# A mixed projection's seven products kept in one slot, instead of two of them being issued in the next slot

## The reference

```
n = rms_norm_2(h, mix_norm_g[l])
q, k, v, qi, ki, wi, xr, yg, cv, gt = split(n @ w_in[l])
attn = dsa_attention(...)             # index scores, top-k, softmax attention
rnn  = rg_lru_branch(xr, yg, ...)     # short conv, gates, scan
cnv  = conformer_conv_branch(cv, ...) # 31 taps, layer norm, silu
g_attn, g_rnn, g_conv = split(sigmoid(gt))
merged = g_attn * (attn @ w_o_attn) + g_rnn * (rnn @ w_o_rnn) + g_conv * (cnv @ w_o_conv)
h = h + merged @ w_out
h = h + (silu(f @ w_gate) * (f @ w_up)) @ w_down      # f = rms_norm_2(h, ffn_norm_g[l])
```

## Time and profile before

| | |
|---|---|
| time, median of 3 runs | 1772.97 us (1772.41 to 1773.33) |
| the profiled execution: its own time | 1771.53 us |
| its span, first to last instruction | 1769.7 us |
| TensorE busy | 1710.7 us, 97% of the span |
| VectorE busy | 1123.0 us, 63% |
| GpSimd busy | 620.6 us, 35% |
| ScalarE busy | 544.5 us, 31% |
| mean granted clock of TensorE | 0.987 |

### The profile page before, as it was taken

One profiled execution on the slowest core, in us unless ns is written; L12 is line 12 of the kernel. 1 busy time (PEld: TensorE's weight loads), 2 busy tenths in 40 slices (PEclk: granted clock), 3 DMA queues, 4 the chain that ended last, 5 costly groups with the idle time before them and its releaser, 6 DMA issues.

```text
span 1769.7 us, 35538 instructions
## 1 busy us (share of the span) xinstructions
PE 1710.7 (97%) x14578; PEld 1457.2 (82%) x14578; DVE 1123.0 (63%) x2020; ACT 544.5 (31%) x1218; POOL 620.6 (35%) x553
## 2 busy tenths in 40 slices
PE   6999998899999999999999999999999997999999
PEld 3344654898888988877899999989888887999999
DVE  2225435566457878979657664368888887667643
ACT  2122236344343355432422010143454304130100
POOL 0002300564106313204644555245123036545652
PEclk9999999899999999999999999999999999999999
DMA  8322300000144434433344444444343343445543
GB/s 323 128 95 95 119 24 1 3 4 4 67 176 143 146 129 156 142 115 125 120 147 164 167 161 158 162 147 161 119 146 121 139 147 116 151 165 172 172 164 108
DMA packets 53377, 225.68 MB, mean 128 GB/s; under 512 B 5088, under 2 KB 29024, under 8 KB 29280
## 3 DMA queue, kind: packets, MB, share of 16 engines
q1 hardware_dynamic: 53216, 223.40, 36.5%
HBM read 222.34 MB, written 1.05 MB: 126 GB/s over the span
## 4 chain that ended last, share of the span: by engine, by line
PE 88%; DVE 6%; ACT 2%; DVEq 1%; issue 1%; DMA 1%; SPq 0%; ACTq 0%
PE PS L748 18%; PE PS L705 15%; PE PS L1013 14%; PE PS L2528 9%; PE PS L1037 8%; PE PS L2025 2%; DVE arena L1420 2%; PE PS L2038 2%; PE PS L687 1%; PE PS L2621 1%; PE PS L865 1%; DMA ring<-stream_dram 1%; PE PS L828 1%; PE PS L977 1%; PE PS L843 1%
## 5 line engine op out<-in xcount | busy, mean ns | idle before, releaser
L748 PE MATMUL PS<-arena,ring 128*128 128x272 f32 (+1 forms) x1664 | 390.0, 389 | 0.4 <-DVE arena L1648 0.4
L748 PEld LDWEIGHTS PS<-arena,ring 128*128 128x128 f32 x1664 | 311.6, 190 | 59.8 <-issue 6.1
L1420 DVE SCALAR_TENSOR_TENSOR arena<-arena,par 128x272 f32<-128x272 f32 (+1 forms) x480 | 258.7, 597 | 6.7
L1860 POOL TENSOR_TENSOR arena<-ring 128x512 f32<-128x512 f32 x48 | 68.8, 1433 | 444.5 <-DMA ring<-stream_dram 355.6
L705 PE MATMUL PS<-arena,ring 128*128 128x136 f32 (+1 forms) x1536 | 202.2, 280 | 1.3 <-ACT arena L1123 1.3
L705 PEld LDWEIGHTS PS<-arena,ring 128*128 128x128 f32 x1536 | 192.9, 191 | 8.0 <-ACT arena L1123 1.7
L2528 PE MATMUL PS<-arena,ring 128*128 128x512 f32 (+2 forms) x448 | 158.2, 514 | 1.7 <-DVEq L2851 1.7
L1013 PE MATMUL PS<-arena 128*128 128x136 f32 (+1 forms) x1280 | 152.1, 277 | 0.0
L705 PE MATMUL PS<-arena 128*128 128x136 f32 (+1 forms) x1152 | 147.8, 280 | 4.3 <-ACT arena L1103 3.0
L1013 PEld LDWEIGHTS PS<-arena 128*128 128x128 f32 x1280 | 148.7, 191 | 0.0
L2528 PEld LDWEIGHTS PS<-arena,ring 128*128 128x128 f32 (+1 forms) x448 | 84.0, 189 | 75.0 <-issue 69.5
(11 more groups left out here) (394 smaller groups left out, 2759.7 us busy)
## 6 DMA issues: line engine op xcount, KB each, us to landing
ring<-stream_dram SPq DMA_DIRECT2D x185, 1024.0 KB, 4.9
ring<-stream_dram SPq DMA_DIRECT2D x32, 512.0 KB, 4.0
ring<-stream_dram SPq DMA_DIRECT2D x16, 384.0 KB, 3.9
arena<-x_dram SPq DMA_DIRECT2D x1, 2048.0 KB, 11.7
cst<-const_dram SPq DMA_DIRECT2D x1, 1080.0 KB, 7.7
out_dram<-H SPq DMA_DIRECT2D x4, 256.0 KB, 3.4
cst<-const_dram SPq DMA_DIRECT2D x1, 912.0 KB, 10.1
arena<-stream_dram SPq DMA_DIRECT2D x1, 512.0 KB, 8.0
```

The costliest lines, as they stand in the source:

```text
L748: last = mm(PS[:, 2 * (j % 2) + f, nw], w[:, k, P * f:P * f + P], src[:, k, nw], start=k == 0, stop=k == KD - 1)
L1420: stt(CVG[:, c, NQ], CVA[:, c, j + Q0:j + T2], dw_w[l][:, c, j:j + 1], CVG[:, c, NQ], ALU.mult, ALU.add)
L1860: g.tensor_tensor(to[:, 0], w21, w22, ALU.add).then_inc(L["summed"], 1)
```

## The change

All seven products of a mixed slot are issued in that slot. TensorE's list in it is now a, g, c, h, then what `within(j)` holds, then e, b, d, in both layers. Exactly one other product stands between a copy and the product that reads on: `g` between `a` and `c`, `c` between `g` and `h`, `h` between `c` and `e`, `b` between `e` and `d`. On ScalarE the copies of `e` and `d` go to the end of the slot, behind all of its other work. VectorE's and GpSimd's lists are as before. The wait for the fourth conv half moves with `e` from slot 43 to slot 42.

```
-        PRODUCTS = counted([[("a", j), *last_parts(j - 1, "e"), ("g", j), ("c", j), *last_parts(j - 1, "d"), ("b", j)]
...
+        PRODUCTS = counted([[(name, j) for name in (("a", "g", "c", "e", "b", "d") if j in MIXED else ("f0", "f1"))]
+                            for j in range(MIXES)])
...
                 if j in MIXED:
                     product_a(j)
-                    if j == OC_J + 1:
-                        pe.wait_ge(L["conv_halves"], B["conv_halves"] + 4)
-                    if j - 1 in MIXED:
-                        product_e(j - 1)
...
                     product_c(j)
-                    if j - 1 in MIXED:
-                        product_d(j - 1)
+                    product_h(j)
                     within(j)
-                    product_h(j)
+                    if j == OC_J:
+                        pe.wait_ge(L["conv_halves"], B["conv_halves"] + 4)
+                    product_e(j)
                     product_b(j)
+                    product_d(j)
...
                 else:
-                    plain(j, 0, range(4))
-                    if j - 1 in MIXED:
-                        product_e(j - 1)
-                    plain(j, 0, range(4, 8))
-                    if j - 1 in MIXED:
-                        product_d(j - 1)
+                    plain(j, 0, range(8))
                     within(j)
                     plain(j, 1, range(8))
-            product_e(MIXES - 1)
-            product_d(MIXES - 1)
...
                 if j in MIXED:
                     copy_a(j)
-                    if j - 1 in MIXED:
-                        copy_e(j - 1)
                     copy_g(j)
                     copy_c(j)
-                    if j - 1 in MIXED:
-                        keep_d(j - 1)
...
                 if j >= WO_J + 2:
                     gain(j - 2)
+                if j in MIXED:
+                    copy_e(j)
+                    keep_d(j)
             gain(MIXES - 2)
-            copy_e(MIXES - 1)
-            keep_d(MIXES - 1)
             gain(MIXES - 1)
```

More of the change, by code:

```diff
@@ L417, in counted @@
             return {key: i + 1 for i, key in enumerate(key for row in rows for key in row)}
-        def last_parts(j, *names):
-            return [(name, j) for name in names if j in MIXED]
         def f0_at(j):
@@ L429, in f1_at @@
             return 2 * MIXED.index(j) + 2
-        PRODUCTS = counted([[("a", j), *last_parts(j - 1, "e"), ("g", j), ("c", j), *last_parts(j - 1, "d"), ("b", j)]
[L433 to L439, removed]
+        PRODUCTS = counted([[(name, j) for name in (("a", "g", "c", "e", "b", "d") if j in MIXED else ("f0", "f1"))]
+                            for j in range(MIXES)])
+        COPIES = counted([[(name, j) for name in (("a", "g", "c", "e", "d") if j in MIXED else
+                                                  () if j in BRANCH or j >= WO_J else ("f0", "f1"))]
+                          for j in range(MIXES)])
         LAYER_COUNTS = dict(
@@ L1239, in scalar_layers @@
                     copy_a(j)
-                    if j - 1 in MIXED:
-                        copy_e(j - 1)
                     copy_g(j)
                     copy_c(j)
-                    if j - 1 in MIXED:
-                        keep_d(j - 1)
[L1246 to L1252, removed]
+                elif j not in BRANCH and j < WO_J:
+                    keep_plain(j, 0)
                 if j in (GA_J, GA_J + 1):
```

## The result

The changed kernel takes 1801.78 us (median of 4 runs, 1801.19 to 1803.0) against 1772.89 us before, a ratio of 1.016 with a 95% interval of 1.0146 to 1.0174: 28.9 us slower. The profiled execution has a span of 1801.1 us, 31.4 us more than before; the difference of the medians is smaller, since the profiled execution of before lies 1.4 us under its median and that of after (1803.0 us) 1.2 over.

The account below looks back on a forecast made before the run. TensorE, busy 97% of the span, was taken as the bound. Terms 8.3 + 10.5 + 0.9 + 3.4 - 1.1 = 22.0 us, plus 2.4 for the clock, on 1771.53 gave 1796; with 1.44 for the median, 1797.5 us; range 1786 to 1804.

Parts of the forecast that it names:

- The formula from rows of before: Wait of d for ScalarE's work beyond the free cover, slots 5 to 24: 8.3 us layer 0, 10.5 layer 1.
- One product between a copy and its reader: All mixed slots: costs nothing where ScalarE is free, with 0.40 of 0.93 us to spare.
- Waits added ahead are not paid back: Against the rival that waits in slots 39 and 37 shrink by all they have: -8.7 us, 1789, chance 0.13.
- The entry of the list: TensorE's total wait behind the copy of e: from 1.3 to about 20 us, longest 3 to 4 us.
- The step on slots 5 and 7: d waits for the rectifier and squares in slot 5, 1.3 us, and the sigmoid in slot 7, 0.65; both layers.
- that rival: ScalarE is held longer at a table load than its row says, with a copy queued behind: 1811, chance 0.01.
- I expect the clock to stay up: -1.6: Slots 38 to 42, layer 0: d cuts the 2.57 us pause in pieces, so 1.6 us of lost clock is saved.
- I take two falls at 1.2: +2.4: Clock falls after new waits in slots 24, 40 and 42: 2.4 us in all, bounds 0 and 8.
- My rival of the clock: Clock falls at each wait of 2 us and more (slots 11, 24, 40, 42): 8.0 us, 1803, chance 0.13.
- 1.1 us for b as a cover: End of both layers, slot 49: b covers d's wait for e's copy, -1.3 us, less 0.2 for the gains.
- My bound for the gains: Gains of slot 48 coming behind d's copy, end of a layer: bounded at 0 to 1.3 us, taken at 0.2.
- c of slot 42 was to wait for the copy of a: Slot 42's copies queue behind d's copy of 41, held until slot 40 is gated: +0.9 us layer 0, +3.4 layer 1.

Follow-up runs that it names:

- experiment 1: Changed kernel with the copy of e moved ahead of or into ScalarE's other work in the nine slots where d waited: 1783.86 us, ratio 1.0058.
- experiment 2: Changed kernel with e and d of those nine slots issued in the next slot, as before the change: 1783.3 us, ratio 1.0047.
- experiment 4: Changed kernel with the buffer of a mixed slot's weights given back as late as before the change: 1800.17 us, ratio 1.0145.
- experiment 3: Kernel before with slot 24 alone changed: 1781.24 us, ratio 1.0045.
- experiment 9: Changed kernel, e's copies earlier, buffers held, slots 41 to 44 in old order, slot 48's gain earlier, GpSimd waiting for VectorE's squares: 1770.47 us, ratio 0.9985.
- experiment 6: Kernel before with slot 49 alone changed, and the gain of slot 48 between the copies of e and d there: 1773.82 us.
- experiment 5: Kernel before with slot 49 alone changed: 1774.76 us.
- experiment 8: Kernel of experiment 6 with slot 41's copy of a and slot 40's copy of e taken after the fourth of eight silu: 1775.36 us, ratio 1.0013.

## Why the prediction was right, and where it was not

The forecast was 24.5 us slower, the result is 28.9. Its mechanism is the one that acts, and its size is off by terms that partly cancel: 9.2 us that I had too low against 2.4 that I had too high. Without the 2.4 the time would have come out at 1804, the edge of my range, so that it lies 2 us inside it is in part luck.

**Right as it stood.** ScalarE's other work ahead of the copy of e makes d wait, in the nine slots named and in no other (experiments 1 and 2). The formula from rows of before gave 3.15 and 3.65 us for slot 24, and the listed waits with 0.27 added are 3.16 and 3.64; 1.75 and 1.75 for slots 18 and 21 of layer 1, measured 1.75 and 1.73; 0.9 for slots 18 and 21 of layer 0, measured 0.71 and 0.69; 2.05 for slot 11 of layer 0, of which 0.65 is paid back in slot 13, measured 1.78 + 0.27 = 2.05 and a step of 1.21. One product between a copy and its reader costs nothing where ScalarE is free. Waits added ahead are not paid back in slot 37 of layer 1 (5.97 us against 6.14). The entry of the list was to grow to about 20 us and grew to 29.0, 9.6 of it in slots 38 to 40.

**The step on slots 5 and 7.** I wrote of slot 5 that c's copy "stays there (as many products lie ahead of it as before)". That was wrong: d of the slot before now lies ahead of it too, and the copy came at 576.09, not 574.92 (0.24 of these 1.17 us came from ahead of slot 2, the other 0.93 is that product). In slot 5 of layer 0 this cancelled, since the rectifier moved with it (1.26 us against 1.3). But VectorE's scores hang on the rectifier, and the sigmoid of slot 7 on VectorE: it was not fixed in time, as I took it. In layer 1 the rectifier waits 0.80 us for VectorE, so that slot 5 lost 2.00 us and not layer 0's 1.3. Slot 7 lost 1.90 and 1.75 us where I had 0.65. Part of that is a second thing, in the timeline of the changed kernel:

```profile
591.02 1.27 POOL L1840 TENSOR_TENSOR ring<-ring 128x512 f32<-128x512 f32 x1
591.07 1.37 DVE L1508 TENSOR_TENSOR arena<-arena 128x136 f32<-128x136 f32 x1
...
592.52 1.28 ACT L1159 ACT_TABLE_LOAD   x1 [1.92 <-DVE arena L1508]
...
593.81 0.66 ACT L1159 ACTIVATE arena<-arena 128x544 f32<-128x544 f32 x1
```

VectorE's addition, on which the sigmoid waits, took 1.37 us beside GpSimd; with the buffers held (experiment 4) it took 0.29, and the wait was 0.37 us shorter. Together the two slots account for 3.0 us of what was missed. The sigmoid again starts 0.01 us after its table load, so that rival stays out.

**The clock.** "I expect the clock to stay up: -1.6" came true, the fall behind slot 39 went. "I take two falls at 1.2: +2.4" was mis-sized: four new ones came, in slots 24 and 40 of both layers, and lost 8 us together. In slot 24 they cost 4.84 - 3.16 = 1.7 and 6.46 - 3.64 = 2.8 us; experiment 3 shows them with slot 24 changed alone (4.74 - 3.16 = 1.6 and 5.32 - 3.64 = 1.7). In slot 40 they lost 1.7 us each; the wait in slot 42 that was to hide them isn't there, and they are part of the step from 38 to 47. Slot 24 alone is 2.1 us over the whole term. My rival of the clock, with 8.0 us and 1803, was nearer in size than the forecast: four of its five falls came and cost as much. Its rule doesn't hold, though: the wait of 2.31 us in slot 37 of layer 0 left the clock at 1.00.

**What I left out.** I followed the copies and not the ring. d in its own slot frees the weights' buffer earlier, the transfer and GpSimd's sums of weights come earlier, and before slot 37 of layer 0 they fall on VectorE's taps: 2.6 us (experiment 4). At the end of a layer I credited 1.1 us for b as a cover; it came out at a loss of 0.4, because TensorE, 0.95 us earlier there (the old wait of 0.68 at d, and 0.27), releases GpSimd into VectorE's additions (experiment 9). My bound for the gains was beside the point (experiment 6).

**Too high.** c of slot 42 was to wait for the copy of a, 2 to 3 us in layer 1. In the changed kernel it doesn't wait at all; in experiments 1 and 2, with the waits at d gone, it waits 3.2 to 3.7 us. The queue behind the copy of d of 41 is real, but VectorE gated slot 40 early enough in the changed kernel. Its last addition there in layer 1, first before, then after:

```profile
1506.19 1.60 DVE L1648 TENSOR_TENSOR arena<-arena 128x512 f32<-128x512 f32 x1
```

```profile
1533.30 0.69 DVE L1623 TENSOR_TENSOR arena<-arena 128x512 f32<-128x512 f32 x1
```

It lies 27.1 us later, while the copy of c of slot 42 lies 32.5 us later (1538.23 against 1505.71): held back in slot 40, TensorE also held back GpSimd's sums, which wait for its products, and VectorE ran alone. I read this from the two timelines; no run here isolates it. So 38 to 47 cost 3.1 us, not 4.3, in spite of the two falls of the clock. The lists of TensorE's waits there say why it is so little: the new ones, 4.84 us in layer 0 and 4.79 in layer 1, took the place of old ones of 4.44 (2.57, 1.46 and 0.41) and 4.24 (1.49, 1.51 and 1.24).

Misses of 3.0 (slots 5 and 7), 2.1 (clock of slot 24 over 2.4), 2.6 (slot 37) and 1.5 (layer ends) and of -1.2, -0.55 and -0.65 (38 to 47, 27 to 38 of layer 1, slots 11, 18 and 21) make 6.8, which is 31.2 less the forecast's 24.4.

## What to carry to other kernels

When a product is moved closer to the copy that it needs, ask what else stands in the copying engine's list between the two: its length against the cover left gave what the wait costs within 0.2 us in slots 11, 18, 21 and 24 of both layers, and moving that one copy up takes it away again (29.0 us of waits, experiment 1). Then follow each resource that the moved instruction gives back, not only what it waits for: an earlier free buffer started an earlier transfer, and cost 2.6 us before one slot. A cover that is gained just ahead of another engine's wait is often only a shorter wait there (experiments 5 and 8).

## What the runs showed of the hardware

**VectorE and GpSimd hold each other up.** An addition of VectorE with both inputs in SBUF takes 0.29 or 0.30 us for 136 columns alone and 1.14 and 1.37 in the rows above beside a sum of GpSimd, and ends there about 0.15 us after GpSimd's instruction; for 512 columns it takes 0.69 us alone and 1.60 beside one. Between 530 and 1590 us of the changed kernel's trace 26 additions of these two sizes took longer than alone, and every one overlaps an instruction of GpSimd; the 44 that overlap none all take 0.29 to 0.30 or 0.69 us. It goes the other way too: GpSimd's fourth sum takes 1.27 us at 591.02 in the trace after and 1.72 at 1505.52 in that of before, where it starts during an addition of VectorE (1.76 us from 1504.36). An addition with one input in PSUM isn't touched: 0.44 us at 844.74 (L1500), while GpSimd adds from 844.65 to 845.94, and the same in all 116 of that size, 55 of which overlap GpSimd. The Trainium skill ("SBUF — State Buffer", SBUF: two separate sides) says that a VectorE instruction with two SBUF inputs and a GpSimd instruction that reads SBUF take one pair of ports by an exclusive lock for the whole instruction; the traces agree. I had not thought that a change on TensorE would shift the two against each other by enough to matter; it cost about 5 us here (2.6 before slot 37, 1.0 and 0.8 at the ends of the layers, 0.6 in the two slots 7); that it gave something back in slot 40 is read from the timelines alone.

**A wait of the same length may or may not bring the clock down.** Over the eleven traces, waits of TensorE of 2.3 to 2.7 us in the slots were followed by a granted clock at the 1.2 GHz level in 3 cases of 11, waits of 2.9 to 3.7 us in 13 of 14, and the one of 5.6 to 6.1 us in slot 37 of layer 1 in all. The 2.57 us of slot 39, which I took for a length that does it, are 2.58 to 2.60 in experiments 2, 5, 6 and 8, and there the clock stays up. A fall's length differs too: the one in slot 24 of layer 1 cost 2.8 us in the changed kernel and 1.7 in experiment 3, behind the same wait of 3.37 us. What tells the cases apart stays open.
